# A hybrid recurrence and attention block: the last mixer turn splits four of its eight recurrence rows in its loop and four behind it, and the first four merge sums are made in two parts

## Chip, cores and metric

The kernel runs on one core of one Trainium2 chip. The metric is the device time of one execution in microseconds, median of several; lower is better. All tensors are float32. A float32 product is made of three TensorE passes: each operand is split into a high part (fp32r, a cast by ScalarE) and a low part (the rest, a subtraction by VectorE), and high x high, high x low and low x high are summed in a PSUM bank.

## Reference, cut to what matters

```python
y_rnn_x = h_x * jax.nn.gelu(gx)                 # gated recurrence, 1024 channels x 1024 tokens
y_na_x = neighborhood_attention(...)            # 16 heads of 64
...
merged = jax.nn.sigmoid(g_rnn) * (y_rnn @ w_rnn_out) + jax.nn.sigmoid(g_na) * (y_na @ w_na_out)
return merged @ w_out
...
x = x + mx[2] * merge_branches(y_rnn_x, y_na_x, mrx, mnx, w_rnn_out[l], w_na_out[l], w_out[l])
x = x + mx[5] * conv_ffn(modulate(x, ...), ...)
```

The change touches `y_rnn @ w_rnn_out`: its operand y_rnn is held transposed, as eight rows k of 128 channels x 1024 tokens, and an output unit n of 128 channels is a sum over all eight rows.

## The kernel before

**Mixer.** Eight turns i = 0 to 7 handle 128 channels each: projections, the recurrence, whose result is stored to DRAM (`yr_d`), and the attention of two heads. The attention is a loop over 16 units u (`ATT`), a block of queries of one head each. In a unit, TensorE transposes the probabilities into PSUM (L953, L958, `prob_transposes`), ScalarE casts them to the high part (`probT_high`, L1165), VectorE subtracts for the low part (`probT_low`, L1494), takes the reciprocal of the sums (`inverse`, L1503, which also waits for the scores of unit u+2), and makes the masked scores and maxima of unit u+2 (`maxima`, L1482 to L1489), which ScalarE exponentiates (`prob`, L1155). Between, TensorE makes the scores of unit u+2 (L935 to L940) and, every other unit, the weighted values of group g (`weighted_values`, L973 and L991), for which ScalarE copies half away (`bottoms`, L1171) and VectorE writes `yT` (`outputs`, L1508 and L1511). `weighted_values(g)` waits for `outputs(g-1)`, and the transposes of a unit wait for `probT_low` of the unit before. The orders on each engine are written out by hand; the DMA queue of SyncE (SP) is in order as well, and a wait on it holds all that stands behind.

**The last turn.** Since all of `yr_d` is there by then, the loop of turn 7 also prepares the merge: SP loads row k of it into one of two buffers `raw[:, k % 2]` (`load_y`, L704) once row k-2 has been split (`y_lo` counts rows); ScalarE (`y_high`, L1175) and VectorE (`y_low`, L1465) split one row at each odd u. `mix_high` and `mix_low` (L1180, L1472) split the first two blocks of `w_mix` at u = 2 and 6. TensorE adds row (u - 5) / 2 to the first merge sum (`mix_piece`, L1001 to L1003, three matmuls of 512 columns) at u = 5, 7, ..., 15; rows 6 and 7 follow around the last weighted values.

**Merge.** 24 units n of two halves (512 tokens each), 24 matmuls a half (`three_passes`, L47 to L49), in three phases of eight: y_rnn, attention, w_out. Sums go to banks 7, 0, 1, 2 in turn. The first sum is the one that the mixer made, so the merge's TensorE starts with unit 0, half 1. Unit n's weights come by SP into `raw[:, n % 2]` (L1681 for n = 2 and 3, waiting until rows 6 and 7 of y have been split, as they lie in the same buffers; L1693 after), are cast by ScalarE (L1780) and completed by VectorE (L1804), once the sum that used the slot is full. Behind w_mix[2] and w_mix[3], SP loads two blocks of `w_modT` (L1683, L1688) and the broadcast rows `sc` (L1689). VectorE first makes the low part of w_mix[2], then waits for `sc` after its Silu on ScalarE (L1789), and only then multiplies the first sum (L1828), which frees its bank; unit n, half h, waits for `free` to reach 2n + h - 3. GpSimd waits for all rows of y and for the last store of `yT`, zeroes a tile (L1710) and issues the loads of `aux` and `ys`, two each at first.

**FFN.** Behind the merge; untouched.

Of the kernel before, what the change touches and what calls it, by code (L numbers as in the profile page):

```python
# [52 lines left out]
def build(nc, xT, ctxT, svec, c_rows, w_modk, w_shiftT, w_modT, b_mod, gains, w_fm, w_qkv, lru_w, lru_p, qk_g, rpb,  # L53
          w_mix, w_ff, w_down, ffn_p, consts, outT, yr_d, yn_d, smr_d, smn_d, x1_d, h_d, bias_d, down_d):
    with ExitStack() as top:
# [39 lines left out]
        with ExitStack() as cd:  # L95
# [6 lines left out]
            with ExitStack() as rest:  # L102
                sbuf(rest, "rest_of_tokens", [P, 2 * KC * C])
                mixer_sync, mixer_pool, mixer_pe, mixer_act, mixer_dve, mixer_over = mixer_programs(
                    nc, sem, sbuf, w_fm, w_qkv, lru_w, qk_g, rpb, bias_d, consts, w_mix,
                    eps, lrup, decay, xnh, xnl, qh, ql, weights, banks, yh, yl, yr_d, yn_d, smr_d, smn_d, mix_first)
# [360 lines left out]
CHUNKS = ((0, 2 + NT // 2), (2 + NT // 2, Q_TILES))  # L467


def mixer_programs(nc, sem, sbuf, w_fm, w_qkv, lru_w, qk_g, rpb, bias_d, consts, w_mix,  # L470
                   eps, lrup, decay, xnh, xnl, qh, ql, weights, banks, yh, yl, yr_d, yn_d, smr_d, smn_d, mix_first):

    with ExitStack() as st:
        raw, fh, fl, raw_in, w_hi, w_lo = weights
        mix_in, mix_hi, mix_lo, mix_full = mix_first
# [195 lines left out]
        def sync(sp):  # L671
# [34 lines left out]
            def turn(i, first, last):  # L706
# [38 lines left out]
                else:  # L745
# [9 lines left out]
                    for k in range(2, KC):  # L755
                        sp.wait_ge(y_lo, k - 1)
                        load_y(k)
                        if k == 3:
                            sp.wait_ge(mix_lo, 1)
                            sp.dma_start(raw[:, 2, :], w_mix[1]).then_inc(mix_in, 16)  # L760
                        if k in (5, 6):
                            store_y(i, k - 5)
                    store_y(i, 2)
# [93 lines left out]
        def tensor(pe):  # L857
# [137 lines left out]
            def mix_piece(k):  # L995

                if k == 0:
                    pe.wait_ge(mix_lo, 1)
                    pe.wait_ge(f_free, f_count(PAIRS - 1, LAST_MN + 1))
                pe.wait_ge(y_lo, k + 1)  # L1000
                pe.matmul(F_ps, fh[:, 0, k, :], yh[:, k, 0:HALF], start=(k == 0), stop=False)  # L1001
                pe.matmul(F_ps, fh[:, 0, k, :], yl[:, k, 0:HALF], start=False, stop=False)
                done = pe.matmul(F_ps, fl[:, 0, k, :], yh[:, k, 0:HALF], start=False, stop=(k == KC - 1))  # L1003
                if k == KC - 1:
                    done.then_inc(mix_full, 1)

            def turn(i, first, last):
# [59 lines left out]
                for u in range(ATT):  # L1067
# [3 lines left out]
                    if last and u % 2 == 1 and u >= 5:  # L1071
                        mix_piece((u - 5) // 2)
# [11 lines left out]
            mix_piece(KC - 2)  # L1084
            weighted_values(PAIRS - 1, GROUPS_ATT - 1)
            mix_piece(KC - 1)

        def scalar(act):
# [111 lines left out]
            def turn(i, first, last):  # L1200
# [89 lines left out]
                for u in range(ATT):  # L1290
# [12 lines left out]
                    elif u % 2 == 1:  # L1303
                        y_high(u // 2)
                    elif u in (2, 6):
                        mix_high(u // 4)
# [4 lines left out]
            turn(PAIRS - 1, False, True)  # L1311
            bottoms(PAIRS - 1, GROUPS_ATT - 1)

        def vector(dve):
# [199 lines left out]
            def turn(i, first, last):  # L1514
# [66 lines left out]
                for u in range(ATT):  # L1581
# [6 lines left out]
                    if last:  # L1588
                        if u % 2 == 1:
                            y_low(u // 2)  # L1590
                        elif u in (2, 6):
                            mix_low(u // 4)
                    elif u == 4:
                        split_low(G, i)
                if last:
                    outputs(i, GROUPS_ATT - 1, False)
                if first:
# [7 lines left out]
        return sync, gpsimd, tensor, scalar, vector, (yr_out, stage_out, yn_out, y_lo, bound_done)  # L1605
# [11 lines left out]
def merge_programs(nc, sem, sbuf, xT, w_mix, w_ff, c_rows, w_modT, bm, mod, sc, total, x1, x1_d, yh, yl, yn_d, smr_d,  # L1617
# [3 lines left out]
    with ExitStack() as st:  # L1621
# [8 lines left out]
        yr_out, stage_out, yn_out, yr_lo, scores_read = mixer_over  # L1630
# [101 lines left out]
        def tensor(pe):  # L1732
            for ph in range(3):
# [6 lines left out]
                def block_pair(r):  # L1740
                    for b in range(2):
# [17 lines left out]
                        for half in range(2):  # L1759
                            if n == 0 and half == 0:  # L1760
                                continue
                            if n == 0:
                                pe.wait_ge(scores_read, PAIRS * ATT)
                            if n >= 2:
                                pe.wait_ge(free, n * 2 + half - 3)
# [1068 lines left out]
```

## Time and profile before

| what | value |
|---|---|
| median of 3 runs | 2133.04 us (2132.55, 2133.04, and one of 7922.56) |
| the profiled execution | 2128.76 us |
| its span, first to last instruction | 2126.9 us |
| TensorE busy | 2051.1 us (96%) |
| VectorE busy | 1628.0 us (77%) |
| ScalarE busy | 1072.5 us (50%) |
| mean granted TensorE clock | 0.997 |

PE is TensorE, PEld its weight loads, DVE VectorE, ACT ScalarE, POOL GpSimd, SP SyncE and SPq its DMA queue. Times in a timeline are microseconds from the start of the span. "banks" stands for all PSUM; L12 is line 12 of the kernel before. A row's end in the trace overlaps the next row's start a little on PE, DVE and ACT, as these are pipelined, so spacing is read from start to start.

### The profile page before, as it was taken

To read this page: it belongs to the slowest core of one execution; us is meant where nothing else is said; L and a number is where in the kernel's file an instruction comes from. 1 tells how busy PE (TensorE), PEld (TensorE's weight loads), DVE (VectorE), ACT (ScalarE), POOL (GpSimd) and SP (SyncE) were. 2 spreads that over 40 slices of the span, in tenths; PEclk is the share of its full clock that TensorE was granted. 3 is DMA by queue.
4 is the path that set the end of the run, shared out by engine and by line. 5 is a ranking of instruction groups with operands and counts; after the bars stand their busy time and mean duration, and the time that the engine had idled before them with its cause. 6 is when DMAs were issued, how large, how long until landed. Compare 5 with 4: busy or idle time off the path is not lost.

```text
span 2126.9 us, 28320 instructions
## 1 busy us (share of the span) xinstructions
PE 2051.1 (96%) x10618; PEld 1739.8 (82%) x10618; DVE 1628.0 (77%) x2809; ACT 1072.5 (50%) x1631; POOL 492.8 (23%) x377
## 2 busy tenths in 40 slices
PE   5999999999999999999998899999999999999999
PEld 1878888988988889888887788887788888887887
DVE  6688598596885985859859866767998888877766
ACT  3466666665676657656666621002444334434332
POOL 0031130222212212212123010000124442115550
PEclk9999999999999999999999999999999999999999
DMA  8421211112012120120111385453347764239663
GB/s 328 112 64 41 62 51 47 47 53 70 30 41 72 40 73 20 53 70 30 43 50 69 106 310 193 144 188 131 89 134 197 183 176 118 94 122 335 226 205 126
DMA packets 105576, 241.65 MB, mean 114 GB/s; under 512 B 27264, under 2 KB 32768, under 8 KB 104960
## 3 DMA queue, kind: packets, MB, share of 16 engines
q1 hardware_dynamic: 74304, 191.08, 26.4%
q0 software_dynamic: 14592, 44.05, 8.0%
q10 hardware_dynamic: 16544, 4.72, 1.0%
q8 instruction: 84, 1.38, 0.3%
q14 instruction: 52, 0.43, 0.1%
HBM read 203.11 MB, written 63.96 MB: 126 GB/s over the span
## 4 chain that ended last, share of the span: by engine, by line
PE 77%; DVE 13%; ACT 4%; issue 2%; ACTq 0%; DVEq 0%
PE banks L47 14%; PE banks L49 14%; PE banks L48 14%; PE banks L991 4%; PE banks L862 4%; PE banks L864 4%; PE banks L863 4%; PE banks L895 3%; PE banks L2269 3%; PE banks L2270 3%; PE banks L2271 3%; DVE probT_low L1494 2%; PE banks L953 2%; DVE prob L1486 2%; PE banks L935 1%
## 5 line engine op out<-in xcount | busy, mean ns | idle before, releaser
L47 PE MATMUL banks<-qh,xnh 128*128 128x384 f32 (+1 forms) x640 | 223.3, 349 | 0.3 <-PEq L216 0.3
L862 PE MATMUL banks<-xnh,wh 128*128 128x512 f32 (+1 forms) x536 | 211.3, 394 | 3.2 <-ACT stage L1097 2.9
L49 PE MATMUL banks<-qh,xnl 128*128 128x384 f32 (+1 forms) x640 | 207.7, 325 | 0.0
L48 PE MATMUL banks<-ql,xnh 128*128 128x384 f32 (+1 forms) x640 | 207.6, 324 | 0.0
L864 PE MATMUL banks<-xnh,wl 128*128 128x512 f32 (+1 forms) x536 | 204.5, 381 | 0.0
L863 PE MATMUL banks<-xnl,wh 128*128 128x512 f32 (+1 forms) x536 | 204.1, 381 | 0.0
L1494 DVE TENSOR_TENSOR probT_low<-banks,probT_high 128x512 fp32r<-128x512 f32 (+2 forms) x256 | 138.9, 583 | 56.2 <-ACT probT_high L1165 55.2
L1165 ACT CAST probT_high<-banks 128x512 fp32r<-128x512 f32 (+2 forms) x256 | 117.0, 510 | 60.3 <-PE banks L953 51.4
L47 PE MATMUL banks<-yh,wh 128*128 128x512 f32 x372 | 145.0, 390 | 0.9 <-DVE wl L2471 0.9
L48 PE MATMUL banks<-yl,wh 128*128 128x512 f32 x372 | 145.0, 390 | 0.0
L49 PE MATMUL banks<-yh,wl 128*128 128x512 f32 x372 | 144.9, 390 | 0.0
L1362 DVE TENSOR_REDUCE ssq<-sqs 128x4 f32<-128x256 f32 (+1 forms) x80 | 31.0, 389 | 141.5 <-ACT sqs L1107 141.0
L803 POOL TENSOR_TENSOR stage<-stage,one 128x512 f32<-128x512 f32 x32 | 39.0, 1217 | 417.8 <-ACT stage L1097 417.8
L813 POOL TENSOR_TENSOR rstd<-rstd,power 128x24 f32<-128x24 f32 (+1 forms) x16 | 58.9, 3680 | 312.3 <-DVE rstd L1400 312.3
L2106 POOL TENSOR_TENSOR conv_d<-conv_d 128x1024 f32<-128x1024 f32 x22 | 69.1, 3141 | 262.8 <-ACT conv_d L2340 201.0
L1155 ACT ACTIVATE prob<-prob,stat 128x768 f32<-128x768 f32 (+1 forms) x128 | 128.2, 1002 | 2.5 <-DVE stat L1489 2.5
L47 PEld LDWEIGHTS banks<-qh,xnh 128*128 128x128 f32 x640 | 120.8, 189 | 9.0 <-issue 8.1
L48 PEld LDWEIGHTS banks<-ql,xnh 128*128 128x128 f32 x640 | 120.8, 189 | 8.3 <-issue 7.6
L49 PEld LDWEIGHTS banks<-qh,xnl 128*128 128x128 f32 x640 | 120.7, 189 | 0.0
L1780 ACT CAST wh<-raw 128x1024 fp32r<-128x1024 f32 x22 | 23.2, 1055 | 189.4 <-PE banks L49 158.9
L864 PEld LDWEIGHTS banks<-xnh,wl 128*128 128x128 f32 x536 | 101.3, 189 | 19.7
L862 PEld LDWEIGHTS banks<-xnh,wh 128*128 128x128 f32 x536 | 101.7, 190 | 17.3 <-issue 3.0
(396 smaller groups left out, 6015.9 us busy)
## 6 DMA issues: line engine op xcount, KB each, us to landing
raw<-w_ff SPq DMA_DIRECT2D x33, 512.0 KB, 5.7
down_d<-w_down POOLq DMA_DIRECT2D x66, 256.0 KB, 6.9
raw<-w_fm SPq DMA_DIRECT2D x32, 512.0 KB, 6.7
extras<-h_d SPq DMA_DIRECT2D x55, 256.0 KB, 3.9
raw<-w_qkv SPq DMA_DIRECT2D x24, 512.0 KB, 3.9
raw<-w_mix SPq DMA_DIRECT2D x24, 512.0 KB, 4.8
h_d<-conv_d SPq DMA_DIRECT2D x21, 512.0 KB, 3.2
raw<-w_modT SPq DMA_DIRECT2D x16, 512.0 KB, 4.6
```

What stands on the lines that cost most here:

```text
L47: pe.matmul(out, w_hi(k), x_hi(k), start=(k == 0), stop=False)
L48: pe.matmul(out, w_hi(k), x_lo(k), start=False, stop=False)
L49: last = pe.matmul(out, w_lo(k), x_hi(k), start=False, stop=(k == chunks - 1))
L862: pe.matmul(out, fh[:, s, k, :], xnh[:, k, c0:c1], start=(k == 0), stop=False)
L863: pe.matmul(out, fh[:, s, k, :], xnl[:, k, c0:c1], start=False, stop=False)
L864: return pe.matmul(out, fl[:, s, k, :], xnh[:, k, c0:c1], start=False, stop=(k == KC - 1))
L895: pe.matmul(f_bank(j)[:, 0:c1 - c0], lw[:, 2 * (n // 3) + d, :], xc[:, c0:c1], start=True, stop=True).then_inc(f_full, 1)
L991: last = pe.matmul(dst, vS[:, s, h, :], moving, start=(n == 0 and part == 0), stop=(n == len(blocks) - 1 and part == 1))
L1155: act.activation(p, p, ACT.Exp, bias=stat[:, u, 1:2], scale=-1.0, accum_out=stat[:, u, 2:3]).then_inc(exp_done, 1)
L1165: act.copy(probT_blocks(pth, u, bank), probT_bank(u, bank)).then_inc(pt_hi, 1)
L1494: dve.tensor_tensor(probT_blocks(ptl, u, bank), probT_bank(u, bank), probT_blocks(pth, u, bank).bitcast(F32), ALU.subtract).then_inc(pt_lo, 1)
L2106: pool.tensor_tensor(ca, ca, cg, ALU.mult).then_inc(gated, 1)
```

## The change

- `y_high` and `y_low` are called at u = 1, 5, 9 and 13 (rows 0 to 3). Rows 4 and 5 follow behind the loop ahead of the last `bottoms` and `outputs`, rows 6 and 7 behind these.
- `mix_piece` at u = 5, 7, 11 and 15 adds rows 0 to 3 to the first sum. Behind the loop, rows 0 to 3 are added to the sum of unit 0, half 1; then come the last weighted values, then rows 0 to 3 of both halves of unit 1.
- The merge starts with a new function, `first_rest`, which adds rows 4 to 7 to the four sums, one after another, and marks each full.
- On SP, w_mix[1] is loaded behind row 2 of y instead of row 3, and the stores of `yT` stand behind rows 2, 3 and 4 instead of 5, 6 and 7.

```diff
+Y_EARLY = 4
+Y_UNITS = (1, 5, 9, 13)
+MIX_UNITS = (5, 7, 11, 15)
...
                     for k in range(2, KC):
                         sp.wait_ge(y_lo, k - 1)
                         load_y(k)
-                        if k == 3:
+                        if k == 2:
                             sp.wait_ge(mix_lo, 1)
                             sp.dma_start(raw[:, 2, :], w_mix[1]).then_inc(mix_in, 16)
-                        if k in (5, 6):
-                            store_y(i, k - 5)
-                    store_y(i, 2)
+                        if k < 5:
+                            store_y(i, k - 2)
                     store_y(i, 3)
...
-            def mix_piece(k):
-
+            def mix_piece(n, half, k):
+
+                cols = slice(HALF * half, HALF * half + HALF)
+                out = every[:, (7, 0, 1, 2)[2 * n + half], :]
                 if k == 0:
-                    pe.wait_ge(mix_lo, 1)
-                    pe.wait_ge(f_free, f_count(PAIRS - 1, LAST_MN + 1))
+                    pe.wait_ge(mix_lo, n + 1)
+                    if n == 0 and half == 0:
+                        pe.wait_ge(f_free, f_count(PAIRS - 1, LAST_MN + 1))
+                    else:
+                        pe.wait_ge(bound_done, PAIRS * ATT)
                 pe.wait_ge(y_lo, k + 1)
...
-                    if last and u % 2 == 1 and u >= 5:
-                        mix_piece((u - 5) // 2)
+                    if last and u in MIX_UNITS:
+                        mix_piece(0, 0, MIX_UNITS.index(u))
...
-            mix_piece(KC - 2)
+            for k in range(Y_EARLY):
+                mix_piece(0, 1, k)
             weighted_values(PAIRS - 1, GROUPS_ATT - 1)
-            mix_piece(KC - 1)
+            for half in range(2):
+                for k in range(Y_EARLY):
+                    mix_piece(1, half, k)
...
-                    elif u % 2 == 1:
-                        y_high(u // 2)
+                    elif u in Y_UNITS:
+                        y_high(Y_UNITS.index(u))
...
+            for k in range(Y_EARLY, Y_EARLY + 2):
+                y_high(k)
             bottoms(PAIRS - 1, GROUPS_ATT - 1)
+            for k in range(Y_EARLY + 2, KC):
+                y_high(k)
...
-                        if u % 2 == 1:
-                            y_low(u // 2)
+                        if u in Y_UNITS:
+                            y_low(Y_UNITS.index(u))
...
                 if last:
+                    for k in range(Y_EARLY, Y_EARLY + 2):
+                        y_low(k)
                     outputs(i, GROUPS_ATT - 1, False)
+                    for k in range(Y_EARLY + 2, KC):
+                        y_low(k)
...
+            def first_rest(n, half):
+                cols = slice(HALF * half, HALF * half + HALF)
+                for k in range(Y_EARLY, KC):
+                    pe.wait_ge(yr_lo, k + 1)
+                    pe.matmul(ps(2 * n + half), wh[:, n, k, :], yh[:, k, cols], start=False, stop=False)
+                    pe.matmul(ps(2 * n + half), wh[:, n, k, :], yl[:, k, cols], start=False, stop=False)
+                    last = pe.matmul(ps(2 * n + half), wl[:, n, k, :], yh[:, k, cols], start=False, stop=(k == KC - 1))
+                last.then_inc(full, 1)
...
                         for half in range(2):
-                            if n == 0 and half == 0:
+                            if n < 2:
+                                first_rest(n, half)
                                 continue
-                            if n == 0:
-                                pe.wait_ge(scores_read, PAIRS * ATT)
-                            if n >= 2:
-                                pe.wait_ge(free, n * 2 + half - 3)
+                            pe.wait_ge(free, n * 2 + half - 3)
```

## Rows read from the trace of the kernel before

**Rows 1.** The page: busy TensorE, and its granted clock in 40 slices.
```profile
PE 2051.1 (96%) x10618; PEld 1739.8 (82%) x10618; DVE 1628.0 (77%) x2809; ACT 1072.5 (50%) x1631; POOL 492.8 (23%) x377
...
PEclk9999999999999999999999999999999999999999
```

**Rows 2.** Windows: length, busy PE, PEld, DVE, ACT, POOL, clock, DMA.
```profile
1159.00:1213.00 54.00, 43.73 (x306) 38.11 (x305) 50.98 (x143) 40.81 (x79) 1.43 (x2) 1.00 0.24 81
1213.00:1232.00 19.00, 19.00 (x91) 16.04 (x92) 6.53 (x10) 5.75 (x6) 3.30 (x5) 1.00 0.72 262
```

**Rows 3.** Waits of TensorE, whole span: total us, times, longest.
```profile
PE banks L973 <- DVE yT L1511: 12.5, 35, 1.2
PE banks L953 <- DVE probT_low L1494: 12.0, 10, 1.8
PE banks L307 <- DVE xnl L442: 5.8, 1, 5.8
...
PE banks L2269 <- DVE wl L2643: 1.1, 1, 1.1
```

**Rows 4.** Timeline of TensorE: start, us, instruction, idle before and releaser.
```profile
1176.03 0.28 PE L940 MATMUL banks<-kcX,qpS 128*128 128x256 f32 x1
...
1209.70 0.63 PE L953 MATMUL banks<-cst,prob 128*128 128x128 f32 x4 [0.21 <-DVE probT_low L1494]
...
1212.94 0.43 PE L973 MATMUL banks<-cst,stat 128*128 128x128 f32 x2 [1.00 <-DVE yT L1511]
...
1215.34 0.39 PE L47 MATMUL banks<-yh,wh 128*128 128x512 f32 x1
...
1231.66 0.39 PE L47 MATMUL banks<-yh,wh 128*128 128x512 f32 x1
```

**Rows 5.** Timeline of VectorE in the loop of the last turn.
```profile
1171.77 1.21 DVE L1465 TENSOR_TENSOR yl<-raw,yh 128x1024 fp32r<-128x1024 f32 x1
...
1176.42 0.16 DVE L1503 RECIPROCAL stat<-stat 128x1 f32<-128x1 f32 x1
...
1191.75 0.17 DVE L1503 RECIPROCAL stat<-stat 128x1 f32<-128x1 f32 x1 [0.19 <-PE banks L940]
...
1204.33 1.02 DVE L1494 TENSOR_TENSOR probT_low<-banks,probT_high 128x512 fp32r<-128x512 f32 x2 [0.24 <-ACT probT_high L1165]
...
1212.47 0.41 DVE L1511 TENSOR_TENSOR yT<-bot,banks 64x256 f32<-64x256 f32 x1
```

**Rows 6.** Timeline of ScalarE.
```profile
1174.45 0.97 ACT L1165 CAST probT_high<-banks 128x512 fp32r<-128x512 f32 x2 [0.29 <-PE banks L953]
...
1227.44 1.06 ACT L1789 ACTIVATE sc<-sc 128x1024 f32<-128x1024 f32 x1 [4.11 <-DMA sc<-c_rows]
```

**Rows 7.** DMA issues of 1160 to 1290 us, median us to landing.
```profile
raw<-yr_d SPq DMA_DIRECT2D x6, 512.0 KB, 3.3
...
sc<-c_rows SPq DMA_DIRECT2D x1, 512.0 KB, 8.6
```

**Rows 8.** Timeline of the SP queue.
```profile
1216.52 0.93 SPq L1681 DMA_DIRECT2D raw<-w_mix  x2
...
1218.79 0.60 SPq L1689 DMA_DIRECT2D sc<-c_rows  x1
```

**Rows 9.** Timeline of VectorE in the merge.
```profile
1228.53 0.69 DVE L1828 TENSOR_TENSOR x<-banks,aux 128x512 f32<-128x512 f32 x1 [5.24 <-ACT sc L1789]
...
1238.57 1.23 DVE L1804 TENSOR_TENSOR wl<-raw,wh 128x1024 fp32r<-128x1024 f32 x1
...
1249.86 1.23 DVE L1804 TENSOR_TENSOR wl<-raw,wh 128x1024 fp32r<-128x1024 f32 x1 [1.81 <-ACT wh L1780]
```

**Rows 10.** Timeline of GpSimd.
```profile
1218.31 0.95 POOL L1710 MEMSET total_x<- 128x1024 f32 x1 [57.80 <-DMA yn_d<-yT]
```

**Rows 11.** The tile `ys` in 1155 to 1270 us, its loads.
```profile
DMA to landing us min/median/max: 4.2/6.9/10.0
```

**Rows 12.** Windows at the start of the span, columns as in rows 2.
```profile
50.00:60.00 10.00, 3.72 (x20) 3.28 (x21) 9.45 (x19) 4.12 (x4) 0.00 (x0) 0.70 0.01 2
```

More of the change, by code:

```diff
@@ L105, in build @@
                     nc, sem, sbuf, w_fm, w_qkv, lru_w, qk_g, rpb, bias_d, consts, w_mix,
-                    eps, lrup, decay, xnh, xnl, qh, ql, weights, banks, yh, yl, yr_d, yn_d, smr_d, smn_d, mix_first)
+                    eps, lrup, decay, xnh, xnl, qh, ql, weights, banks, every, yh, yl, yr_d, yn_d, smr_d, smn_d, mix_first)
             with ExitStack() as stream:
@@ L467 @@
 CHUNKS = ((0, 2 + NT // 2), (2 + NT // 2, Q_TILES))
+Y_EARLY = 4
+Y_UNITS = (1, 5, 9, 13)
+MIX_UNITS = (5, 7, 11, 15)
 def mixer_programs(nc, sem, sbuf, w_fm, w_qkv, lru_w, qk_g, rpb, bias_d, consts, w_mix,
-                   eps, lrup, decay, xnh, xnl, qh, ql, weights, banks, yh, yl, yr_d, yn_d, smr_d, smn_d, mix_first):
+                   eps, lrup, decay, xnh, xnl, qh, ql, weights, banks, every, yh, yl, yr_d, yn_d, smr_d, smn_d, mix_first):
     with ExitStack() as st:
         raw, fh, fl, raw_in, w_hi, w_lo = weights
-        mix_in, mix_hi, mix_lo, mix_full = mix_first
+        mix_in, mix_hi, mix_lo, _ = mix_first
         with ExitStack() as rnn:
@@ L993, in weighted_values @@
                 last.then_inc(pv_done, 1)
-            def mix_piece(k):
+            def mix_piece(n, half, k):
+                cols = slice(HALF * half, HALF * half + HALF)
+                out = every[:, (7, 0, 1, 2)[2 * n + half], :]
                 if k == 0:
-                    pe.wait_ge(mix_lo, 1)
-                    pe.wait_ge(f_free, f_count(PAIRS - 1, LAST_MN + 1))
-                pe.wait_ge(y_lo, k + 1)
[L1001 to L1005, printed above, removed]
+                    pe.wait_ge(mix_lo, n + 1)
[3 more added lines that the diff above has]
+                        pe.wait_ge(bound_done, PAIRS * ATT)
+                pe.wait_ge(y_lo, k + 1)
+                pe.matmul(out, fh[:, n, k, :], yh[:, k, cols], start=(k == 0), stop=False)
+                pe.matmul(out, fh[:, n, k, :], yl[:, k, cols], start=False, stop=False)
+                pe.matmul(out, fl[:, n, k, :], yh[:, k, cols], start=False, stop=False)
             def turn(i, first, last):
@@ L1604, in vector @@
             turn(PAIRS - 1, False, True)
-        return sync, gpsimd, tensor, scalar, vector, (yr_out, stage_out, yn_out, y_lo, bound_done)
+        return sync, gpsimd, tensor, scalar, vector, (yr_out, stage_out, yn_out, y_lo)
 def mod_column(dve, n, b, row, sc, dots, bm, mod, dotted, mod_done, count):
@@ L1629, in merge_programs @@
         square = sbuf(st, "square_c", [P, HALF])
-        yr_out, stage_out, yn_out, yr_lo, scores_read = mixer_over
+        yr_out, stage_out, yn_out, yr_lo = mixer_over
         _, w_hi, w_lo, full = mix_first
```

## Prediction

> **What bounds the kernel now.** I read the page first: TensorE is busy 96% of the span at an almost full clock [rows 1]. So the time is TensorE's work plus the few places where it waits, and the reader looks for those. The windows by stretch show one such place around the change: in the loop of the last turn (1159 to 1213 us) TensorE is busy 43.7 of 54 us and VectorE 51.0, while from 1213 us on TensorE is busy all the time [rows 2]. The list of who waited says for whom: in all loops together, for VectorE's `yT` and `probT_low` above all [rows 3]. So the loop is a ring of VectorE and TensorE, and the merge behind it is TensorE alone. Behind the loop the longest wait of TensorE is 1.1 us (L2269, in the FFN) [rows 3]: an early delay of the merge has next to nothing to be absorbed in, and a gain passes through as well.
>
> **Unit costs.** The 72 matmuls between 1215.34 and 1231.66 us [rows 4] take 16.32 us, 0.2267 us each; a part of one row (three matmuls) is 0.68 us, a group of 24 is 5.44 us. A row's low split on VectorE is 1.2 us [rows 5]; its high split on ScalarE, a cast of the same tile, I take at the 1.06 us of the Silu over 1024 columns [rows 6].
>
> **The loop.** Rows leave u = 3, 7, 11 and 15; parts of sums leave u = 9 and 13. If VectorE's queue set every unit, three splits (the fourth has nothing of the loop behind it) would give 3 x 1.2 = 3.6 us. But they sit in the units where the ring goes through TensorE, so I follow each.
> - u = 3: without the split, `probT_low` of unit 5 still waits for ScalarE's high part of it, which starts at 1174.45 and has two halves of 0.49 us [rows 6]; with a delay of 0.1 us it starts at 1175.1. The reciprocal behind it waits for the scores of unit 7, whose last matmul starts at 1176.03 for 0.28 us [rows 4]; it ran at 1176.42 [rows 5]. Gain 0.07 us.
> - u = 7: `probT_low` of unit 9 again waits for ScalarE. The reciprocal behind it waited 0.19 us for TensorE, until 1191.75 [rows 5]: VectorE itself was ready at 1191.56. With no part of a sum in unit 9 the scores end 0.68 us earlier, and VectorE is what is late next, at 1191.56 - 0.07 - 0.07 = 1191.42. Gain 0.33 us in all.
> - u = 11: `probT_low` of unit 13 waited 0.24 us for ScalarE [rows 5], which waited for TensorE's transposes; these stand behind the weighted values, which start when `yT` is done. No more gain. The part missing in unit 13 shortens scores that ended about when `probT_low` did: nothing.
> - u = 15: the split there is behind everything that the loop needs.
> The splits kept, at u = 5, 9 and 13, are the ones on the chain, and stay on it. Bounds for the loop: 0 and 3.6 us; I take 0.33, since a row says at each place who was waited for.
>
> **Behind the loop, TensorE.** Before: the transposes of unit 15 start at 1209.70, six matmuls follow, then a wait of 1.00 us for `yT`, the weighted values from 1212.94, three matmuls, 72 from 1215.34 on, and unit n = 2 of the merge starts at 1231.66 [rows 4]: 21.96 us. After: the transposes (0.60), 3 + 12 matmuls (3.40), weighted values (1215.34 - 0.68 - 1212.94 = 1.72), 24 + 48 matmuls (16.32): 22.04 us. The twelve new matmuls ahead of the weighted values fill that wait, and six more stand outside the loop; together +0.08 us. The banks ask for nothing new: the maxima, which read the scores, all stand ahead of outputs(6) on VectorE. TensorE is then ready for n = 2 at 1231.66 + 0.08 - 0.33 = 1231.4.
>
> **Behind the loop, the rows.** With the loop 0.33 us earlier, outputs(6) ends near 1212.5 (before: 1212.47 + 0.41 [rows 5]), so row 4 is split low at 1213.65 and row 5 at 1214.8 (its load is asked for when row 3 has been split at u = 13, 3.5 us earlier, where such a load takes 3.3 us [rows 7]; ScalarE then has it at 1212.9). Loads of rows 6 and 7 wait for these: 1213.7 + 3.3 = 1217.0 and 1214.9 + 3.3 = 1218.2. High and low splits follow one another, 1.05 and 1.2 us: row 6 done at 1219.3, row 7 at 1220.5. TensorE comes to row 4 at 1220.5, to row 6 at 1221.8 and to row 7 at 1222.5. The sum in two parts is thus covered by 24 matmuls of unit n = 1, with 2.0 us to spare; cover gone, each us late costs one. The last outputs wait behind the low split of row 5, but also for the weighted values (1215.3), later anyway: nothing.
>
> **What queues behind row 7.** This is the price. Before, SP's queue was held by the last store of `yT` until 1216.52; then it issued w_mix[2], w_mix[3], two blocks of w_modT and `sc`, the last at 1218.79 [rows 8]. `sc` took 8.6 us to land [rows 7], its Silu ran at 1227.44 [rows 6], and VectorE's first product of the merge (L1828) waited for that, until 1228.53 [rows 9]. n = 2 needs the bank which it frees at 1229.2: 2.4 us of room. After, SP waits for rows 6 and 7: w_mix[2] at 1219.4, w_mix[3] at 1220.6 (before about 1217.0), `sc` 1.8 us behind that as before, 1222.4: 3.6 us later. GpSimd, which also waits for row 7, comes at 1220.6 instead of 1218.31 [rows 10]: 2.3 us later, so its four loads now go out ahead of `sc`. That costs `sc` some 0.65 us of undivided engines, and the earlier w_mix[2] gives about as much back. I take 8.6 us again: it lands at 1231.0, Silu to 1232.1, L1828 at 1232.13 + 0.68, TensorE at 1232.9 where it was ready at 1231.4. TensorE waits 1.5 us; against before, n = 2 starts 1.2 us later. w_mix[2] itself is in time: even with the 8.6 us of `sc` it is there at 1228.0, and split by 1230.3.
>
> Next late: the low weights of n = 3 end 11.3 us behind L1828's start (1239.8 - 1228.53 [rows 9]), needed 11.6 us behind it: just in time. Those of n = 4 (1249.86 + 1.2 [rows 9]) move 3.6 us to 1254.7, needed 96 matmuls behind n = 2, at 1231.66 + 21.76 + 1.2 = 1254.6: a tie, 0.1 us. Each further unit has 48 matmuls, 10.9 us, to hide less than that on VectorE, so the lateness dies out. **Sum**: -0.33 + 0.08 + 1.5 + 0 to 0.1 = +1.2 us. The bounds of the term for `sc` are 0 (landing by 1229.6) and about 3 us (landing in the 10.0 us that was the longest of GpSimd's loads of `ys` [rows 11]).
>
> **One rule weighed.** The trace shows TensorE's granted clock at 1.00, the 2.4 GHz level, in the last loop [rows 2] and at nine tenths or more in each slice of the others [rows 1], though they hold waits of up to 1.8 us [rows 3]; in 50 to 60 us, around the wait of 5.8 us for `xnl` [rows 3], it is 0.70 on average, so partly the 1.2 GHz level [rows 12]. The Trainium skill ("TensorE: Matmul & The Clock Gate", Part 1: The HAM clock gate) says that the clock falls to half after the engine has been idle and comes back once it has been busy. By that rule a long enough new wait in the merge would be paid twice, as the last rival has it; the wait that I forecast is no longer than those that changed nothing here.
>
> **Rivals.**
> - *Covered* (0.2): `sc` lands within 7.1 us, since the SP queue starts on idle engines. For it: w_mix[2] is out 1.2 us ahead. Against: 8.6 us before. Only the loop's gain is left: -0.25 us, 2132.8.
> - *Every split counts* (0.1): VectorE's queue, busy 51 of 54 us [rows 2], sets each unit. The loop is 3.6 us shorter; the loads behind it come earlier too, `sc` is then 0.3 us later than before for 3.6, and n = 2 starts at 1229.6: -2.0 us, 2131.0. Against: the waits for TensorE and ScalarE in [rows 5].
> - *Slower, a chain of late loads* (0.17): the loads of rows 6 and 7, now close together and beside the store of `yT`, take 1.2 us more, and `sc` 10.0 us: 1.2 + 1.2 + 1.4 = +3.8 us, 2136.8. It decides from the point where row 7 is split later than 1222.5; from there the matmuls themselves wait too. For it: nine loads of 512 KB share the engines here. Against: while rows 6 and 7 come, nothing else but a small store is on its way.
> - *Slower, the clock falls* (0.03): the wait at n = 2 grows past the 1.8 us that were harmless, towards the 5.8 that were not. The clock's deficit in [rows 12] was 10 x 0.30 = 3 us; with a wait of 4 us in place of 1.5 that is 1.2 + 2.5 + 3 = +6.7, 2139.7.
>
> **Numbers.** The profiled execution is 2128.76 us (span 2126.9), 4.3 below the median of the runs, 2133.04; the difference is added to that median. The forecast, +1.2, has a chance of 0.5: 2134.2 us. Range: from the rival at 2131.0 with one us for the scatter of executions, 2130, to the late loads with the same, 2138. About 2% is what a measurement of this kernel can tell from no change; no case comes near 43 us, so faster by over 2% 0.01, within 0.98, slower 0.01.
>
> **What would show it.** Right: in the loop of the last turn outputs on VectorE end 0.3 us earlier, not 3.6; no wait of TensorE ahead of rows 4 to 7 (in the lines of the new function); `sc` issued near 1222.4, L1828 waiting for Silu until about 1232; a wait of TensorE of 1 to 2 us at the first L47 of n = 2, clock 1.00. Wrong: TensorE without a wait there, a loop over 1 us shorter, or a wait on `yl` in the merge.

## The result, and the profile after

The changed kernel takes 2135.98 us (median of 13 runs, 2133.60 to 2139.15), the kernel before in the same comparison 2131.66 us (13 runs, 2129.11 to 2133.04, but for one of 7922.56). The ratio is 1.0024, interval [1.0017, 1.0032]: 5.1 us slower by the ratio (3.6 to 6.8), where +1.2 had been forecast. The change of the time is one eighth of the 2% that the verdicts go by.

Single executions of either kernel scatter by 4 to 7 us, and much of that lies ahead of the change: in the profiled executions the last loop starts between 1158.7 and 1163.8 us. So places inside one trace are compared from the start of that loop, the first `probT_low` of turn 7 (1159.30 before, 1161.39 after; line numbers of the changed kernel are 2 to 12 higher in the mixer and 16 to 23 higher behind it).

The timeline of VectorE, changed kernel: start, us, instruction, idle before and what ended it.

```profile
1161.39 1.02 DVE L1506 TENSOR_TENSOR probT_low<-banks,probT_high 128x512 fp32r<-128x512 f32 x2
...
1177.29 1.16 DVE L1506 TENSOR_TENSOR probT_low<-banks,probT_high 128x512 fp32r<-128x512 f32 x2 [0.95 <-ACT probT_high L1173]
...
1192.33 1.16 DVE L1506 TENSOR_TENSOR probT_low<-banks,probT_high 128x512 fp32r<-128x512 f32 x2 [1.10 <-ACT probT_high L1173]
...
1205.97 1.02 DVE L1506 TENSOR_TENSOR probT_low<-banks,probT_high 128x512 fp32r<-128x512 f32 x2 [1.38 <-ACT probT_high L1173]
...
1222.52 1.23 DVE L1477 TENSOR_TENSOR yl<-raw,yh 128x1024 fp32r<-128x1024 f32 x1 [1.24 <-ACT yh L1183]
...
1236.50 0.69 DVE L1851 TENSOR_TENSOR x<-banks,aux 128x512 f32<-128x512 f32 x1 [6.09 <-ACT sc L1812]
```

The three splits of 1.2 us that left the inside of the loop are replaced by three waits for ScalarE of 0.95, 1.10 and 1.38 us (before: none, none and 0.24): VectorE idles where it worked before. That is the answer to [rows 5]. The last row is the one to compare with the first of [rows 9]: the first product of the merge comes 75.11 us behind the start of the loop, before 69.23.

The timeline of TensorE, changed kernel, and behind it what it waited for most, over the whole span (us in total, times, longest).

```profile
1211.24 0.63 PE L955 MATMUL banks<-cst,prob 128*128 128x128 f32 x4 [0.21 <-DVE probT_low L1506]
...
1215.36 0.38 PE L975 MATMUL banks<-cst,stat 128*128 128x128 f32 x2
...
1233.12 0.39 PE L1755 MATMUL banks<-yh,wl 128*128 128x512 f32 x1
1237.34 0.77 PE L47 MATMUL banks<-yh,wh 128*128 128x512 f32 x1 [3.83 <-DVE x L1851]
1237.90 0.63 PE L48 MATMUL banks<-yl,wh 128*128 128x512 f32 x1
...
1242.56 0.39 PE L47 MATMUL banks<-yh,wh 128*128 128x512 f32 x1
```

```profile
PE banks L975 <- DVE yT L1523: 10.9, 33, 1.1
...
PE banks L47 <- DVE x L1851: 3.8, 1, 3.8
```

Against [rows 4]: from the loop's start to the transposes of unit 15 it is 49.85 us (before 50.40). The wait of 1.00 us ahead of the last weighted values is gone (1215.36 has none). From those transposes to the end of the four sums it is 22.10 us, as long as before (21.96). Then TensorE waits 3.83 us for a bank, which no row of before has, and its next twelve matmuls (1237.34 to 1242.56) take 5.22 us, most of them 0.43 us apart, where twelve take 2.72 at 0.227: 2.5 us more. The windows of that stretch (length, busy time and count of each engine, clock, DMA) give the granted clock: the next to last but one number falls from 1.00 to 0.57 and 0.75.

```profile
1235.00:1240.00 5.00, 2.66 (x6) 2.16 (x7) 3.46 (x6) 4.10 (x4) 0.00 (x0) 0.57 0.44 137
1240.00:1245.00 5.00, 5.00 (x18) 4.00 (x17) 4.93 (x10) 0.00 (x0) 1.61 (x3) 0.75 0.74 237
```

What the first product waited for, in the timelines of the SP queue and of GpSimd and in the DMA issues of 1210 to 1245 us (size, median us to landing):

```profile
1210.40 7.11 SPq L707 DMA_DIRECT2D raw<-yr_d  x3
1218.52 0.32 SPq L697 DMA_DIRECT2D yn_d<-yT  x1
1221.32 2.80 SPq L1697 DMA_DIRECT2D raw<-w_mix  x2
...
1225.46 0.43 SPq L1705 DMA_DIRECT2D sc<-c_rows  x1
```

```profile
1223.90 0.96 POOL L1726 MEMSET total_x<- 128x1024 f32 x1 [60.80 <-DVE yl L1477]
```

```profile
raw<-yr_d SPq DMA_DIRECT2D x3, 512.0 KB, 4.2
...
sc<-c_rows SPq DMA_DIRECT2D x1, 512.0 KB, 9.9
```

With 2.09 us taken off for the later start, `sc` is asked for at 1223.37 (forecast 1222.4, before 1218.79 [rows 8]) and takes 9.9 us (forecast and before 8.6 [rows 7]).

### The profile page after: what moved, and what is told of

Read it like the earlier page. It is cut to its first block, busy times and chain, and to the rows that moved or that the text cites. A ratio compares the mean times of both kernels' runs of the same rounds, so it can differ in the third digit from the quotient of the medians.

```text
span 2135.2 us, 28324 instructions
## 1 busy us (share of the span) xinstructions
PE 2054.8 (96%) x10618; PEld 1740.9 (82%) x10618; DVE 1628.8 (76%) x2809; ACT 1073.1 (50%) x1631; POOL 498.1 (23%) x377
## 3 DMA queue, kind: packets, MB, share of 16 engines
q8 instruction: 84, 1.38, 0.3%
## 4 chain that ended last, share of the span: by engine, by line
PE 76%; DVE 12%; ACT 4%; issue 2%; DMA 1%; POOL 0%; SPq 0%; ACTq 0%; DVEq 0%; POOLq 0%
PE banks L47 14%; PE banks L49 14%; PE banks L48 14%; PE banks L993 4%; PE banks L864 4%; PE banks L866 4%; PE banks L865 4%; PE banks L897 3%; PE banks L2292 3%; PE banks L2294 3%; PE banks L2293 3%; DVE probT_low L1506 2%; PE banks L955 1%; DVE prob L1498 1%; PE banks L937 1%
## 5 line engine op out<-in xcount | busy, mean ns | idle before, releaser
L47 PE MATMUL banks<-yh,wh 128*128 128x512 f32 x348 | 136.7, 393 | 4.8 <-DVE x L1851 3.8
L48 PE MATMUL banks<-yl,wh 128*128 128x512 f32 x348 | 136.5, 392 | 0.0
L49 PE MATMUL banks<-yh,wl 128*128 128x512 f32 x348 | 136.4, 392 | 0.0
```

What stands on the lines that cost most here:

```text
L47: pe.matmul(out, w_hi(k), x_hi(k), start=(k == 0), stop=False)
L48: pe.matmul(out, w_hi(k), x_lo(k), start=False, stop=False)
L49: last = pe.matmul(out, w_lo(k), x_hi(k), start=False, stop=(k == chunks - 1))
```

## Experiments

All ran against the kernel before, five rounds each, in three sessions. In the table, "to n = 2" is the time from the loop's start to the first matmul of unit n = 2 in the profiled execution, against 72.36 us before; it leaves out what a slow clock costs behind that point. "Half" is the 1.2 GHz level, "full" the 2.4 GHz level. "Dip" means granted clock below 1.00 around units 14 and 15.

| run | ratio [95% interval] | to n = 2 | wait at n = 2 | clock behind it | dip |
|---|---|---|---|---|---|
| changed kernel | 1.0024 [1.0017, 1.0032] | +3.6 | 3.83 | half, 12 matmuls | no |
| e12, again | 1.0019 [1.0010, 1.0028] | +4.3 | 3.37 | half, 13 matmuls | yes |
| e1 sc ahead | 1.0003 [0.9994, 1.0012] | +1.2 | 0.45 | full | yes |
| e2 16 filled | 1.0028 [1.0017, 1.0038] | +4.4 | filled | full | yes |
| e3 sums only | 1.0005 [0.9997, 1.0014] | +0.9 | none | full | yes |
| e4 sc late | 1.0003 [0.9994, 1.0012] | +1.4 | 1.22 | full | no |
| e5 sc and a block late | 1.0013 [1.0004, 1.0021] | +1.7 | 1.49 | full | no |
| e6 splits only | 1.0038 [1.0025, 1.0051] | +9.7 | earlier | half, earlier | no |
| e7 all loads ahead | 1.0015 [1.0007, 1.0023] | +2.4 | 2.58 | full | no |
| e8 as e7, loop busy | 1.0011 [1.0003, 1.0020] | +2.8 | 2.62 | full | no |
| e9 all loads held | 1.0026 [1.0017, 1.0035] | +4.6 | 4.38 | half, from 1 us on | no |
| e10 in order of need | 1.0007 [0.9998, 1.0016] | +0.8 | none | full | yes |
| e11 12 filled | 1.0014 [1.0005, 1.0023] | +3.4 | filled, then 0.89 | full | no |

**e1: `sc` ahead.** In the changed kernel, the SP queue of the merge asks for `sc` first, then for the first block of `w_modT`, and for w_mix[2] and w_mix[3] behind them.

```diff
-            for n in range(2, 4):
-                sp.wait_ge(yr_lo, KC + n - 3)
-                sp.dma_start(raw[:, n % 2, :], w_mix[n]).then_inc(raw_in[n % 2], 16)
-            sp.wait_ge(w_lo, 2)
-            sp.dma_start(rows[1], w_modT[1]).then_inc(rows_in[1], 16)
             sp.wait_ge(yr_out, PAIRS * 16)
...
+            sp.dma_start(sc[:, :], ...).then_inc(c_in, 16)
             sp.dma_start(rows[0], w_modT[0]).then_inc(rows_in[0], 16)
-            sp.dma_start(sc[:, :], ...).then_inc(c_in, 16)
+            for n in range(2, 4):
+                sp.wait_ge(yr_lo, KC + n - 3)
+                sp.dma_start(raw[:, n % 2, :], w_mix[n]).then_inc(raw_in[n % 2], 16)
+            sp.wait_ge(w_lo, 2)
+            sp.dma_start(rows[1], w_modT[1]).then_inc(rows_in[1], 16)
```

> The changed kernel with one thing moved: on the SP queue of the merge, sc and the first w_modT block are asked for right behind the last store of yT, ahead of w_mix[2] and w_mix[3], which wait for rows 6 and 7. Theory (the loss is the lateness of sc): sc is issued some 3 us earlier and no longer behind three loads, lands before TensorE is ready for n = 2, the wait of 3.8 us there and the slow clock behind it are gone, and the time is 0.4 us below the kernel before (-0.55 in the loop, +0.14 behind it), about 5 us below the changed kernel. Rival (the loss is spread: contention, bank order, the two-part sums): within 1 us of the changed kernel, +0.2% against before. A part of the gain can be lost if w_mix[2], now behind two loads, lands after 1231.

`sc` landed in 4.3 us, the wait fell to 0.45 us, the clock behind it stayed full, and the time is back at that of before: 1.0003 against 1.0024, with intervals that do not meet. These two are from different sessions; in the session of e1 it was e2, below, that kept the late loads, with 1.0028 [1.0017, 1.0038]. The second run of the changed kernel (e12, 1.0019 [1.0010, 1.0028]) just touches e1's interval. The last 0.45 us are those of another load, as the rows of TensorE and VectorE in e1 say:

```profile
1236.81 0.47 PE L47 MATMUL banks<-yh,wh 128*128 128x512 f32 x1 [0.45 <-DVE x L1851]
```

```profile
1235.97 0.69 DVE L1851 TENSOR_TENSOR x<-banks,aux 128x512 f32<-128x512 f32 x1 [1.69 <-DMA aux<-smr_d]
```

The 0.4 us below before did not come.

**e2: the wait filled with 16 matmuls.**

```diff
+                            if n == 2 and half == 0:
+                                for _ in range(16):
+                                    pe.matmul(every[:, 3, :], wh[:, 0, 0, :], yh[:, 0, 0:HALF], start=True, stop=True)
                             pe.wait_ge(free, n * 2 + half - 3)
```

> The changed kernel with 16 matmuls more (512 columns, into a bank that nobody reads; they add nothing to the result) between the sums of n = 1 and the wait of n = 2 for its bank. 16 x 0.227 = 3.6 us fit into the wait of 3.8 us. Theory (a part of the loss, 12 matmuls at 0.43 us in place of 0.23, is the clock that falls in the wait): n = 2 starts at the same moment, its matmuls are 0.23 us apart from the first, granted clock 1.00, and the time is 2.5 us below the changed kernel, +2.6 against before. Rival (the clock is no separate term, only the wait counts): same time as the changed kernel, +5, or more where the 16 matmuls outlast the wait.

In the timeline of TensorE the filling does keep the clock up, and it is longer than the wait (the bank was free at 1236.0, n = 2 starts at 1236.67):

```profile
1233.04 3.79 PE L1790 MATMUL banks<-yh,wh 128*128 128x512 f32 x16
1236.67 0.39 PE L47 MATMUL banks<-yh,wh 128*128 128x512 f32 x1
1236.89 0.39 PE L48 MATMUL banks<-yl,wh 128*128 128x512 f32 x1
```

The time is 1.0028, not the forecast +2.6 us (1.0012, outside the interval). This expectation failed; e11 takes it up.

**e3: the sums alone.** TensorE's part of the change, with the splits and SP's order of before.

```diff
-                    elif u in Y_UNITS:
-                        y_high(Y_UNITS.index(u))
+                    elif u % 2 == 1:
+                        y_high(u // 2)
...
-                        if u in Y_UNITS:
-                            y_low(Y_UNITS.index(u))
+                        if u % 2 == 1:
+                            y_low(u // 2)
...
```

> Only TensorE's part of the change: sums in two parts, parts of the first one at u = 5, 7, 11, 15, rest as in the merge of the change; all eight rows are split in the loop, as before, and SP's order is that of before. Theory: TensorE's part alone costs nothing: the loop gains up to 0.2 us at unit 9, the 0.14 us behind it are lost, sc is as early as before, no wait at n = 2: within 0.3 us of the kernel before. Rival (the two-part sums or the other bank order cost time themselves): slower by over 1 us.

1.0005 [0.9997, 1.0014], +1.1 us (-0.6 to 3.0): the timing alone does not decide between the two; in the trace there is no wait at n = 2, but 0.9 us more than before up to it. All of that is a dip of the clock at the loop's end (below), so the sums themselves cost nothing there.

**e4: `sc` late, in the kernel before.**

```diff
+            sp.wait_ge(full, 3)
             sp.dma_start(sc[:, :], ...).then_inc(c_in, 16)
```

> The kernel before with one wait more: the SP queue asks for sc only when the third sum is full (about 1226.3 us for 1218.8); nothing else is touched. Theory (a late sc is enough to make the loss): it lands about 1231.5 to 1232.5, TensorE waits 2.2 to 3.3 us at n = 2: +2 to +3 us if the clock stays at full speed through such a wait, +4.5 to +6 us if it falls as it did in the changed kernel (12 matmuls at half speed, 2.5 us). Rival (sc is covered anyway, the changed kernel lost its time elsewhere): within 0.5 us of before.

Mis-sized: asked for 7.6 us later, `sc` landed in 4.7 us, as the other loads were through, so the wait was 1.22 us and the time 1.0003. In this trace a late single load is not the late block of the changed kernel. The wait of 1.22 us moved the start of n = 2 by 1.4 us and left the clock alone; the timing gives +0.6 us (-1.3 to 2.6).

**e5: a little more.** The same wait, ahead of the first w_modT block as well.

```diff
+            sp.wait_ge(full, 3)
             sp.dma_start(rows[0], w_modT[0]).then_inc(rows_in[0], 16)
             sp.dma_start(sc[:, :], ...).then_inc(c_in, 16)
```

> The kernel before, with SP asking for both the first w_modT block and sc only when the third merge sum is full. In e4 sc alone was asked for there, 8 us later than before, but landed in 4.7 us instead of 8.6 (the loads beside it were through), so TensorE waited only 1.2 us. Two loads instead of one should bring L1828 some 5.5 us later than before (e4: 3.7), a wait at n = 2 of about 3 us. Theory (a late sc alone makes the loss of the changed kernel): +3.3 us where the clock stays, +5.8 where it falls in the wait. Rival (it takes something else in the changed kernel): within 1 us of before although the profile shows the wait.

Again smaller than expected, 1.49 us of wait and +1.7 us up to n = 2; the time, 1.0013 (0.9 to 4.5 us), lies between the two theories and decides neither.

**e6: the splits alone.** The changed kernel with the sums one after another.

```diff
-            for k in range(Y_EARLY):
-                mix_piece(0, 1, k)
             weighted_values(PAIRS - 1, GROUPS_ATT - 1)
-            for half in range(2):
-                for k in range(Y_EARLY):
-                    mix_piece(1, half, k)
...
-                for k in range(Y_EARLY, KC):
+                for k in range(Y_EARLY if n + half == 0 else 0, KC):
                     pe.wait_ge(yr_lo, k + 1)
...
```

> Only the splits of the change: rows 4 to 7 behind the loop, SP's order of the change, but the merge sums one after another (the first one needs rows 4 to 7 right behind the loop, 24 matmuls of unit 1 are no longer ahead of them). Theory (the two-part sums are what hides the late rows): TensorE waits for rows 6 and 7, some 4 and 2 us, then has 72 matmuls to n = 2, where sc is there already: about +7 us against before, +9.5 where the clock falls in the wait. Rival (late rows are cheap, sc is all): no worse than the changed kernel, +5.

The timeline of TensorE shows the two waits for rows 6 and 7 in the first sum, and the first slow matmul, behind the second wait:

```profile
1222.35 0.50 PE L1750 MATMUL banks<-yh,wh 128*128 128x512 f32 x1 [3.22 <-DVE yl L1472]
...
1224.79 0.80 PE L1750 MATMUL banks<-yh,wh 128*128 128x512 f32 x1 [1.47 <-DVE yl L1472]
```

1.0038, and +9.7 us up to n = 2 in the trace, of which the slow clock behind the two waits is 2.6 us (eleven matmuls 0.43 us apart, and the restart): the two-part sums hide what they were said to hide. With them no matmul of the changed kernel waits for a row.

**e7: GpSimd's loads ahead as well.**

```diff
-            pool.wait_ge(yr_lo, KC)
             pool.memset(total[:, :], 0.0).then_inc(zeroed, 1)
...
```

> As e1 (sc and the first w_modT block ahead of w_mix[2] and [3]), and GpSimd no longer waits for row 7 before it zeroes its tile and loads aux and ys; in e1 VectorE's first product waited 1.7 us for aux and TensorE 0.45 us for it. Theory: no wait at n = 2, loop 0.5 us shorter, tail 0.1 longer: 0.4 us below before, 0 to 0.5 us below e1. Rival (the earlier loads of GpSimd slow down those of rows 6 and 7): a wait of TensorE in rows 6 or 7 of the first sum, slower than e1 by up to 1 us.

Wrong, and it shows why the order counts. ScalarE's timeline:

```profile
1234.19 1.05 ACT L1802 CAST wh<-raw 128x1024 fp32r<-128x1024 f32 x1 [9.21 <-DMA raw<-w_mix]
1235.26 1.28 ACT L1811 ACT_TABLE_LOAD   x1
1236.55 1.06 ACT L1811 ACTIVATE sc<-sc 128x1024 f32<-128x1024 f32 x1
```

and the DMA issues of 1215 to 1240 us:

```profile
raw<-w_mix SPq DMA_DIRECT2D x2, 512.0 KB, 9.5
...
sc<-c_rows SPq DMA_DIRECT2D x1, 512.0 KB, 4.4
```

`sc` was there, but its Silu stands behind the cast of w_mix[2]. The loads of w_mix[2] and w_mix[3] took 9.5 us in the median (7.0 in e1), with GpSimd's four asked for in the same two microseconds. The wait came back with 2.58 us. Half of it, 1.28 us, is the table load that ScalarE makes between the cast and the Silu; in the changed kernel it ran at 1229.17, while `sc` was still on its way. The Trainium skill ("DMA: Bandwidth & Descriptors", Queues, rings and completion order) says that each DMA engine takes packets in turn from the queues which have work; the outcome agrees: with GpSimd's loads 2 us earlier against w_mix[2] than in e1, SP's two were 2.5 us slower. How the engines share packets no run shows.

**e8: the loop kept busy.** As e7, with six parts of the first sum in the loop.

```diff
-MIX_UNITS = (5, 7, 11, 15)
+MIX_UNITS = (5, 7, 9, 11, 13, 15)
...
-                        mix_piece(0, 0, MIX_UNITS.index(u))
+                        mix_piece(0, 0, max(MIX_UNITS.index(u) - 2, 0), u < 9)
```

> As e7, with TensorE as busy in the loop as before: six parts of the first sum at u = 5, 7, 9, 11, 13 and 15; those of 5 and 7 start a sum with row 0 that is thrown away, so the result is complete. It is a test of the clock at the end of the loop: in the profiles of e1, e2 and e3, which have no part of a sum in units 9 and 13, the granted clock was 0.5 to 0.7 for some 3 us around the last units, in those of before and e4, with parts there, it was 1.00. Theory (the parts in units 9 and 13 kept the clock up): clock 1.00 at the end of the loop, and time within 0.5 us of e7, as 0.35 us of the loop's gain are given back and up to 1.1 us of slow matmuls saved. Rival (the dips are chance): a dip here too, 0.3 us slower than e7.

Clock 1.00 through the loop, time as e7 within the intervals. But e7's profile has no dip either, so this run alone tells nothing.

**e9: all loads held, in the kernel before.**

```diff
+            sp.wait_ge(full, 2)
             for n in range(2, 4):
                 sp.wait_ge(yr_lo, KC + n - 3)
...
             pool.wait_ge(yr_lo, KC)
+            pool.wait_ge(full, 2)
```

> The kernel before with all loads of the merge held, SP's and GpSimd's, until the second merge sum is full (1220.8 us); rows, loop and sums are those of before. So sc is asked for near 1223.2, where the changed kernel has it (1223.4 after its start is set equal), with the same loads around it. Theory (the loss of the changed kernel is the late block of loads and nothing else): sc lands in 9 to 10 us, L1828 comes about 5.5 us later than before, TensorE waits 3 to 3.8 us at n = 2: +3.4 us where the clock stays, +6 where it falls; the time of the changed kernel within 1.5 us. Rival (part of the loss lies in the loop's end or the two-part sums): at least 2 us faster than the changed kernel in the same session.

This is a loss as large as the changed kernel's without a line of its splits or sums: 1.0026 [1.0017, 1.0035], beside 1.0019 [1.0010, 1.0028] for the changed kernel in the same session (e12). `sc` took 11.2 us, the wait was 4.38 us, and the clock fell about a microsecond behind it:

```profile
1240.18 0.47 PE L47 MATMUL banks<-yh,wh 128*128 128x512 f32 x1 [4.38 <-DVE x L1830]
...
1241.21 0.63 PE L48 MATMUL banks<-yl,wh 128*128 128x512 f32 x1
1241.63 0.63 PE L49 MATMUL banks<-yh,wl 128*128 128x512 f32 x1
```

**e10: loads in the order of need.** SP: `sc`, w_mix[2], w_mix[3], the w_modT blocks; GpSimd: aux[0] at once, the rest behind row 7; ScalarE: the Silu first.

```diff
+            sp.dma_start(sc[:, :], ...).then_inc(c_in, 16)
             for n in range(2, 4):
                 sp.wait_ge(yr_lo, KC + n - 3)
                 sp.dma_start(raw[:, n % 2, :], w_mix[n]).then_inc(raw_in[n % 2], 16)
+            sp.dma_start(rows[0], w_modT[0]).then_inc(rows_in[0], 16)
+            sp.wait_ge(w_lo, 2)
+            sp.dma_start(rows[1], w_modT[1]).then_inc(rows_in[1], 16)
...
-            act.wait_ge(full, 2)
-            w_split(2, 0)
             act.wait_ge(c_in, 16)
             act.activation(sc[:, :], sc[:, :], ACT.Silu).then_inc(c_silu, 1)
+            act.wait_ge(full, 2)
+            w_split(2, 0)
...
+            pool.memset(total[:, :], 0.0).then_inc(zeroed, 1)
+            pool.dma_start(aux[:, 0, :], smr_d[0]).then_inc(aux_in[0], 16)
             pool.wait_ge(yr_lo, KC)
-            pool.memset(total[:, :], 0.0).then_inc(zeroed, 1)
-            for n in range(2):
-                pool.dma_start(aux[:, n, :], smr_d[n]).then_inc(aux_in[n], 16)
+            pool.dma_start(aux[:, 1, :], smr_d[1]).then_inc(aux_in[1], 16)
```

> The changed kernel with the loads in the order of need: SP asks for sc behind the last store of yT, then w_mix[2], w_mix[3], and the two w_modT blocks last; GpSimd zeroes its tile and loads aux[0] at once, the rest of its loads behind row 7 as before; ScalarE does the Silu ahead of the cast of w_mix[2]. In e7 all loads went out early and w_mix[2] took 9 to 10 us; its cast stands ahead of the Silu on ScalarE, so the wait came back (2.6 us). Theory: only three loads are in the way now, sc lands in 4.4 us, w_mix[2] in 6, aux[0] in 5; no wait at n = 2, no low clock: 0 to 0.4 us below before. Rival (the 0.5 us of the loop are lost to clock dips at its end, as in the profiles of e1 to e3): 0.5 us above before with no wait at n = 2.

No wait at n = 2 and VectorE's first product 2.9 us ahead of it, yet 1.0007 [0.9998, 1.0016]: a gain is not shown. The rival fits: a dip at the end of the loop, in TensorE's timeline the four transposes of unit 15 in 1.05 us instead of 0.63:

```profile
1209.84 1.05 PE L955 MATMUL banks<-cst,prob 128*128 128x128 f32 x4
1210.68 0.64 PE L960 MATMUL banks<-cst,prob 128*128 128x128 f32 x2
```

**e11: the wait filled with 12 matmuls**, `range(12)` in the edit of e2.

> As e2 with 12 matmuls instead of 16 in the wait of n = 2 (2.7 us of a wait of 3.8; in e2 the 16 outlasted the wait by some 0.5 us and the time was no better than that of the changed kernel). Theory (in most executions the clock falls in the wait and costs up to 2.5 us behind it): 1 to 2.5 us below the changed kernel in the same session, clock 1.00 in the profile behind n = 2's start. Rival (the clock falls in few executions, the profiled one was one of them): same time as the changed kernel within 1 us.

The clock stayed full again, and the last 0.89 us of the wait are seen. 1.0014 [1.0005, 1.0023] against e12's 1.0019: 0.4 us by the medians (2135.11 and 2135.53), 1 us by the ratios, and the intervals overlap. Neither theory is excluded by the times; what the clocks of the single executions add is told below.

**e12: the changed kernel again.**

> The changed kernel once more, unchanged, for a second profile and for its time in one session with e9 and e11. Expected: 4 to 6 us above before; in the profile a wait of 3 to 4 us at n = 2; the clock behind it open: at half for 12 matmuls if that belongs to the wait, at 1.00 if it was chance.

Second profile, same picture: 3.37 us of wait and thirteen slow matmuls, so by what was written down the slow clock belongs to the wait. Now there is also a dip in the loop. The windows of that dip:

```profile
1206.00:1209.00 3.00, 2.46 (x14) 2.46 (x15) 2.77 (x6) 1.12 (x3) 0.00 (x0) 0.69 0.28 66
1209.00:1212.00 3.00, 3.00 (x15) 2.73 (x15) 1.12 (x4) 2.11 (x4) 0.00 (x0) 0.74 0.45 158
```

## Why the prediction was right, and where it was too small

The direction, the place and the mechanism were right, the size was a quarter of what came: +1.2 us forecast, 5.1 measured. The range held the time, in part by its base: it was laid around 2133.04, the median of three executions; laid around 2131.66 it would end at 2136.6, only 0.6 us above the measured 2135.98. What came is less the case forecast (0.5) than the rival *a chain of late loads* (0.17), whose +3.8 us stand against the +3.6 up to n = 2, with the fall of the clock (0.03) on top. e1 and e9, one taking the late loads out of the changed kernel and one putting them into the kernel before, show that the block of loads held behind row 7 is the loss. No run held only SP's or only GpSimd's part of the block, so their shares are not told apart. Point by point:

- **The loop.** Forecast 0.33 us; the transposes of unit 15 come 0.55 us earlier after the start: 0.10 us were gained by unit 5 and 0.34 in unit 9, close to the forecast, and 0.11 in unit 13, where nothing had been expected. VectorE idles in place of the splits, behind ScalarE at each of the three places that the prediction named. "Every split counts" (3.6 us) is out.
- **Behind the loop, TensorE.** Forecast +0.08 us, measured +0.14. No wait for a row: row 7 is done at 1223.75 - 2.09 = 1221.7, needed at 1222.5 by the forecast. 0.8 us to spare, not 2.0, because the load of row 7 took 4.2 us and that of row 5 4.4, not 3.3 (row 6 did take 3.3). The cover was there, thinner; e6 shows the price without it.
- **The issue of `sc`.** Forecast 3.6 us later than before, measured 4.6. The slower loads of rows 5 and 7 are the difference: w_mix[2], behind row 6, went out in time (1221.32 - 2.09 = 1219.2, forecast 1219.4).
- **The landing of `sc`.** This is the term that was mis-sized most: "I take 8.6 us again". It took 9.9 us. The traces put this beside GpSimd's loads: `sc` landed in 8.6 and 9.0 us where it was asked for 0.4 us ahead of GpSimd's first load (before, e3), in 9.7 to 9.9 where it was asked for 0.7 us behind that load (changed kernel, e2, e6, e11, e12), and in 11.2 where it was 1.0 us behind (e9). These runs differ in more than that, so it is likely and not shown. The prediction has all four of GpSimd's loads ahead of `sc`; in the rows only the two of `aux` were asked for by then (from 1224.79 on, `sc` at 1225.46, `ys` from 1226.13). What it took off for the earlier w_mix[2] did not make them up. Together with the later issue the wait is 3.83 us, not 1.5, and n = 2 starts 3.6 us later, not 1.2. The upper bound given for this term, about 3 us, was itself passed, because it counted the landing only and not the later issue on top.
- **The clock.** The rival with a chance of 0.03 came in: in both profiles of the changed kernel and in e9 the matmuls behind the wait start 0.43 us apart for a while, 2.5 us in all in the first. The prediction tied it to a wait of 4 us, so what was too low is the chance of such a wait; its size, 3 us, was about right. In this kernel waits of 1.2 to 2.6 us (e4, e5, e7, e8) left the clock at 1.00, those of 3.4 to 4.4 us did not, nor did the 3.22 and 1.47 us of e6 with three matmuls between them. With the rule of the Trainium skill that the prediction weighed ("TensorE: Matmul & The Clock Gate", Part 1: The HAM clock gate) this agrees: the clock falls to half after the engine has been idle.
- **n = 3 and n = 4.** No wait of TensorE from 1245 to 1480 us in the changed kernel: the tie held. It is as close as forecast: in e4 and e8 TensorE waits 0.31 and 0.37 us for the low weights at the start of n = 4.

Summed for the first profile: -0.55 + 0.14 + 4.0 (the wait, from start to start) + 2.5 = +6.1 us from the start of the loop. With the 2.1 us by which the loop started later, which is scatter ahead of the change, that is 8.2 of the 8.3 us between the spans (2135.2 and 2126.9). The timed ratio says 5.1 (3.6 to 6.8); 6.1 lies inside.

Open: how much of the timed loss is the slow clock. In the three profiles with a wait of 3.4 us or more it fell each time, and filling the wait kept it up in both profiles (e2, e11), but the timings don't show the 2.5 us that this should save: e2 is no faster than the changed kernel, and e11 is faster by 0.4 to 1 us with intervals that overlap. The filling of e2 outlasted the wait by 0.5 us, which explains a part only. The mean granted clock of every single execution is on record and says a little more. In the mean over the executions it is 0.9945 and 0.9949 for the changed kernel (13 and 11 of them) and 0.9941 in e9 (11), but 0.9951 and 0.9956 where the wait was filled (e2, 8; e11, 11), and 0.9955 to 0.9959 for the kernel before in the three sessions. Between the changed kernel and the filled ones that is 0.0007, good to some 0.0005 by the scatter, or 1.5 us of 2133. It suggests that the clock falls in executions without a profile as well. In how many, and what it costs them, stays open.

## What to carry to other kernels

Moving work out of a busy loop pays only where that work is what the next engine waits for; here it left from the units where the ring ran through ScalarE and TensorE, and 3.6 us of splits gave 0.55. Ask of each step that is moved what its completion count releases on the in-order queues: the last of four splits came 7.6 us later and held nine loads behind it, and the last of these in SP's queue was the one that TensorE ended up waiting for. Such loads are best asked for in the order of need (e1 took the loss back), and a burst of others beside them can undo it (e7). The order of the engine that uses them counts as well: in e7 `sc` was there and its Silu waited for another load's cast.

## What the runs showed of the hardware that was not expected

The clock also fell at the end of the loop, without a long wait. In five of the nine profiles without parts of a sum in units 9 and 13 (e1, e2, e3, e10, e12) the granted clock was 0.5 to 0.9 in windows between 1206 and 1215 us, though no wait of TensorE there is over 1.2 us; in the other four (the changed kernel's first, e6, e7, e11) it was 1.00, and so it was in all five with parts there (before, e4, e5, e8, e9). From the loop's start to the last weighted values it is 55.0 to 55.3 us in the five with a dip and 54.0 in the changed kernel's first profile and e11: 1.0 to 1.3 us, twice what the loop had gained. The clocks of all executions point the same way: in the six runs without those parts and with no wait over 2.6 us left empty (e1, e2, e3, e7, e10, e11) the mean is 0.0003 to 0.0012 below that of the kernel before in the same session, 0.0006 on average or 1.3 us of clock; in the three with them (e4, e5, e8) it is 0.0002 below to 0.0003 above. That the six matmuls missing from units 9 and 13 cause it is likely, not shown: e8, the run made for it, had a kernel without a dip in its profile to compare with. It would explain why e1, e3 and e10, with little or no wait left at n = 2, are not faster than before. No version that beats the kernel before was found.

A load of 512 KB took 3.2 to 12.6 us here depending on what was asked for beside it: `sc` 4.3 to 4.7 us where it went first or alone (e1, e4, e5, e7, e8, e10), 8.6 us before, 9.7 to 11.2 us behind four others with GpSimd's loads beside it (changed kernel, e2, e6, e9, e11, e12).
